# Decoder layer on 8 cores: the mixer's tile loads, tables and out-projection traffic issued from ScalarE's queue, and a second tile buffer for the out-projection

## What is computed

```python
u = modulate(rmsnorm(h, mix_norm), sh2, sc2)
proj = u @ w_in                       # q, k, v of 4 differential heads; latents and k_rope of 4 MLA heads
dq, dk = apply_rope(dq, cos_d, sin_d), apply_rope(dk, cos_d, sin_d)      # tables of 64 columns
kr, q_rope = apply_rope(kr, cos_r, sin_r), apply_rope(q_rope, cos_r, sin_r)  # tables of 32 columns
h = h + g2 * (concatenate([od, om], -1) @ w_out)     # the out-projection
u = modulate(rmsnorm(h, ffn2_norm), sh3, sc3)
h = h + 0.5 * g3 * swiglu(u, w_gate, w_up, w_down)   # D_FF = 2816
```

## Time and profile before

| | us |
|---|---|
| median of 3 executions | 3066.21 (3059.49 to 3182.67) |
| the profiled execution | 3062.68 |
| its span on the slowest core (core 0) | 3061.1 |
| spans of the 8 cores | 3041.2 to 3061.1 |
| PE busy on core 0 | 2843.8 (93%) |
| DVE, ACT busy | 1402.7 (46%), 1255.3 (41%) |

### The profile page before, as it was taken

The page is one execution under the profiler, slowest core; times in us unless marked ns, Lnnn a source line. Parts: engine busy times, 40 slices in busy tenths (PEclk is TensorE's granted clock), DMA queues, the critical chain, the costliest instruction groups (busy, mean ns, idle before and its releaser), DMA issues.

```text
span 3061.1 us, 42691 instructions; the slowest of 8 cores (3041.2 to 3061.1 us)
## 1 busy us (share of the span) xinstructions
PE 2843.8 (93%) x16528; PEld 1355.0 (44%) x16528; DVE 1402.7 (46%) x2808; ACT 1255.3 (41%) x1751; POOL 75.1 (2%) x147
## 2 busy tenths in 40 slices
PE   3999988999899999999978999999999999999998
PEld 1344433444454444544434445544454444444443
DVE  2555215445465445344445545654535444532532
ACT  2421105335434456454235453555755624322311
POOL 1000000000000000000000000000000000000000
PEclk9999999999999999999989999999999999999999
DMA  9678985476924934552793334334245368436446
GB/s 212 116 146 160 201 217 170 125 213 129 205 81 111 180 124 99 121 155 104 234 281 117 97 104 125 111 116 144 75 135 154 119 234 281 138 110 200 165 121 223
DMA packets 144138, 470.76 MB, mean 154 GB/s; under 512 B 17376, under 2 KB 21216, under 8 KB 129760
## 3 DMA queue, kind: packets, MB, share of 16 engines
q1 hardware_dynamic: 127600, 399.80, 41.2%
q0 software_dynamic: 16336, 68.23, 15.0%
HBM read 452.83 MB, written 100.66 MB: 181 GB/s over the span
## 4 chain that ended last, share of the span: by engine, by line
PE 75%; DMA 12%; ACT 5%; DVE 5%; SPq 1%; issue 1%; POOL 0%; ACTq 0%; DVEq 0%; POOLq 0%
PE psall L127 75%; ACT pt L127 3%; DMA hst<-xL 2%; DMA h<-hst 2%; DMA h<-qk 2%; DMA wf<-sdn 2%; SPq L127 1%; DMA wf<-wgu 1%; DMA wf<-w_ada 1%; ACT mu L127 1%; DMA qk<-h 1%; ACT L127 1%; DVE accsb L127 1%; DVE qk L127 1%; DVE mu L127 1%
## 5 line engine op out<-in xcount | busy, mean ns | idle before, releaser
L127 PE MATMUL psall<-uf,wf 128*128 128x512 bf16 x4224 | 1036.7, 384 | 39.7 <-DMA wf<-wgu 13.2
L127 ACT ACTIVATE pt<-psall 128x1024 bf16<-128x1024 f32 (+3 forms) x520 | 452.8, 872 | 458.4 <-PE psall L127 456.9
L127 PEld LDWEIGHTS psall<-uf,wf 128*128 128x128 bf16 x4224 | 399.9, 99 | 472.2 <-issue 36.7
L127 PE MATMUL psall<-actf,wf 128*128 128x512 bf16 x2112 | 514.4, 385 | 16.6 <-DMA wf<-sdn 16.6
L127 ACT ACTIVATE ftf<-psall 128x512 f32<-128x512 f32 x352 | 210.0, 597 | 658.3 <-PE psall L127 638.4
L127 DVE SCALAR_TENSOR_TENSOR ftf<-ftf,psall 128x512 f32<-128x512 f32 x352 | 241.1, 685 | 443.6 <-ACT ftf L127 412.5
L127 PE MATMUL psall<-mu,wm 128*128 128x512 bf16 (+2 forms) x1312 | 328.9, 381 | 13.7 <-ACT mu L127 9.6
L127 PE MATMUL psall<-mixb,wf 128*128 128x512 bf16 x1408 | 323.0, 384 | 9.0 <-ACT mixb L127 6.7
L127 PEld LDWEIGHTS psall<-actf,wf 128*128 128x128 bf16 x2112 | 200.0, 99 | 226.0 <-issue 18.7
L127 DVE SCALAR_TENSOR_TENSOR hst<-psall,SC,hst 128x512 f32<-128x512 f32 x120 | 90.0, 750 | 434.5 <-PE psall L127 260.4
L127 DVE TENSOR_TENSOR actf<-ftf,psall 128x512 bf16<-128x512 f32 x264 | 180.9, 685 | 195.2 <-PE psall L127 192.8
(11 more groups left out here) (113 smaller groups left out, 1993.6 us busy)
## 6 DMA issues: line engine op xcount, KB each, us to landing
wf<-sgu SPq DMA_DIRECT2D x242, 512.0 KB, 4.1
wf<-sdn SPq DMA_DIRECT2D x192, 352.0 KB, 4.2
h<-hst SPq DMA_DIRECT2D x120, 256.0 KB, 4.5
xt<-h SPq DMA_DIRECT2D x30, 1024.0 KB, 7.2
wm<-w_ada POOLq DMA_DIRECT2D x32, 512.0 KB, 11.0
hst<-xL SPq DMA_DIRECT2D x64, 256.0 KB, 7.4
qk<-h SPq DMA_DIRECT2D x16, 1024.0 KB, 6.6
h<-qk SPq DMA_DIRECT2D x16, 1024.0 KB, 9.6
```

The source lines that it names most:

```text
L127: ins = getattr(eng, o.fn[0])(**o.fn[1])
```

## The change

- `load_half` takes an engine. The mixer's loads of tiles 0 to 3 go to ACT's queue. They are not issued at once: `later(n, fn)` puts a function into `posts_m`, and the main loop runs it n lane-M pieces later (`run_posts_m`). Tile 0's halves come 3 and 6 pieces after the mixer's start, the table load 8, tile 1's halves 18 and 21; the prefetches 2 pieces after the piece that frees the half. The lag of the first norm goes from 14 to 20.
- `tables` stores to `tabC`; a new `spread_tab` copies each sample's tables DRAM to DRAM into `tabD` [2, 128, 2, T] and `tabE` [2, 32, 2, T] (8 copies of 128 KB and 4 of 64 KB a sample, on SP, in lane M behind the adaLN products). `load_tab` is then one transfer: 1 MB on ACT, or 256 KB on SP.
- The out-projection has two tile buffers: QK for even tiles, and VA with TAB (`VTP`) for odd ones. Its loads (`oload`) and stores (`ostore`) are on ACT: a store 2 pieces after m = 3 and m = 7, the load of that half for tile tt + 2 five pieces after the store. The ones in VA are written anew by a memset at the start of mixer 1's projection.
- A tile yields 8 x W_OUT, and W_OUT is 1.3 for sample 0 and 0.75 for sample 1; 3 more pieces follow the last tile. The out-projection weights are released two pieces at a time during the last tile.

```diff
-W_OUT = 0.75
+W_OUT = [1.3, 0.75]
...
-    tabD = dscr("tabD", [2, 4, 128, 512], BF16)
+    tabC = dscr("tabC", [2, 128, T], BF16)
+    tabD = dscr("tabD", [2, 128, 2, T], BF16)
+    tabE = dscr("tabE", [2, 32, 2, T], BF16)
...
+        VAF, TABF = VA[:, 0:4096].bitcast(F32), TAB[:].bitcast(F32)
+        VTP = [(VAF[:, k * 512:(k + 1) * 512], vaR) for k in range(4)] + [(TABF[:, k * 512:(k + 1) * 512], tabR[2 * k:2 * k + 2]) for k in range(4)]
+        OUTP = [QKP, VTP]
...
                 if nxt is not None and k % 4 == 3 and nxt[2]():
-                    load_half(pcs, nxt[0], nxt[1], tag, k // 4)
+                    later(2, functools.partial(load_half, pcs, nxt[0], nxt[1], tag, k // 4, (), "act"))
...
+        def later(n, fn):
+
+            posts_m.append([n, fn])
+
+        def run_posts_m(everything=False):
+            due = []
+            for x in posts_m:
+                x[0] -= 1
+                if x[0] <= 0 or everything:
+                    due.append(x)
+            for x in due:
+                posts_m.remove(x)
+                x[1]()
...
+        def spread_tab(s):
+
+            dma_group([tabDR[s]], tabCR[s], f"txd{s}", [(tabD[s, 32 * q:32 * q + 32, si, :], tabC[s, 64 * (1 - si):64 * (1 - si) + 32, :]) for q in range(4) for si in range(2)])
+            yield 6.0
+            dma_group([tabER[s]], tabCR[s], f"txe{s}", [(tabE[s, 16 * q:16 * q + 16, si, :], tabC[s, 32 + 64 * (1 - si):48 + 64 * (1 - si), :]) for q in range(2) for si in range(2)])
+            yield 6.0
...
             if diff:
-                parts = [(slice(32 * r, 32 * r + 32), si, 64 * (1 - si), 32) for r in range(4) for si in range(2)]
+                S.dma("act", r=[tabDR[s]], w=tabR, stream="taba", out=flat, in_=tabD[s])
             else:
-                parts = [(slice(64 + 16 * r, 80 + 16 * r), si, 32 + 64 * (1 - si), 16) for r in range(2) for si in range(2)]
+                S.dma("sp", r=[tabER[s]], w=tabR, stream="tabs", out=flat[64:96], in_=tabE[s])
...
-                                      functools.partial(there, tt), lambda: True, ("mu", s, tt), 14, nxt, True))
-            for tt, pcs, tag in ((0, MIXP, "MIX"), (1, MUS, "MUS")):
+                                      functools.partial(there, tt), lambda: True, ("mu", s, tt), 20, nxt, True))
+            for tt, pcs, tag, n in ((0, MIXP, "MIX", 1), (1, MUS, "MUS", 16)):
                 assert there(tt)
                 for h in range(2):
-                    load_half(pcs, hD[0][s, tt], hR[0][s][tt], tag, h)
+                    later(n + 2 + 3 * h, functools.partial(load_half, pcs, hD[0][s, tt], hR[0][s][tt], tag, h, (), "act"))
+            later(8, functools.partial(load_tab, s, True))
...
+                    if s == 1 and a == 0 and tt == 0:
+                        I("dve", "memset", w=vaR, ap=vaug[:, :, :, 128:129], constant=1.0)
...
+            def ostore(tt, h):
+                ks = range(4 * h, 4 * h + 4)
+                S.dma("act", r=[x for k in ks for x in OUTP[tt % 2][k][1]], w=[hR[1][s][tt][k] for k in ks], stream=f"os{tt % 2}{h}",
+                      out=hD[1][s, tt, :, 4 * h:4 * h + 4, :].rearrange("p k n -> p (k n)"), in_=oflat(tt, h))
+                if h == 1:
+                    flags.add(("h", 1, s, tt))
+                if tt < 2:
+                    later(5, functools.partial(oload, tt + 2, h))
+            for tt in range(2):
+                for h in range(2):
+                    later(2, functools.partial(oload, tt, h))
...
-                    if m in (4, 7):
-                        if m == 7:
-                            yield W_OUT
...
+                    if m in (3, 7):
+                        later(2, functools.partial(ostore, tt, m // 4))
+                    if tt == 3 and m % 2:
+                        wm.release((s, "wo", m // 2))
+                    yield W_OUT[s]
...
+            for _ in range(3):
+                yield W_OUT[s]
...
             for s in range(2):
+                yield from spread_tab(s)
```

More of the change, by code:

```diff
@@ L259, in build @@
         hR = [[[[Res(f"h{i}_{s}_{t}_{k}") for k in range(NK)] for t in range(4)] for s in range(2)] for i in range(3)]
-        tabDR = [[Res(f"tabD{s}_{t}") for t in range(4)] for s in range(2)]
+        tabCR = [[Res(f"tabC{s}_{t}") for t in range(4)] for s in range(2)]
+        tabDR = [Res(f"tabD{s}") for s in range(2)]
+        tabER = [Res(f"tabE{s}") for s in range(2)]
         sguR = [[Res(f"sgu{i}_{j}") for j in range(22)] for i in range(2)]
@@ L359, in dma_group, with load_half @@
                 o.dval = first.dval
[L361 removed]
+        def load_half(pcs, src, srcR, tag, h, after=(), eng="sp"):
             ks = range(4 * h, 4 * h + 4)
@@ L367, in load_half @@
                 out, frm = flat[:, h * 2048:(h + 1) * 2048], src[:, 4 * h:4 * h + 4, :].rearrange("p k n -> p (k n)")
-            o = S.dma("sp", r=[srcR[k] for k in ks] if srcR else [], w=[x for k in ks for x in pcs[k][1]], stream=f"{tag}{h}", out=out, in_=frm)
+            o = S.dma(eng, r=[srcR[k] for k in ks] if srcR else [], w=[x for k in ks for x in pcs[k][1]], stream=f"{tag}{h}{eng}", out=out, in_=frm)
             for q in after:
@@ L765, in tables @@
             yield 2.0
-            S.dma("sp", r=[snR], w=[tabDR[s][tt]], stream="tst", out=tabD[s, tt], in_=sn[:])
+            S.dma("sp", r=[snR], w=[tabCR[s][tt]], stream="tst", out=tabC[s, :, tt * 512:(tt + 1) * 512], in_=sn[:])
+        def spread_tab(s):
[3 more added lines that the diff above has]
+            yield 6.0
         def load_tab(s, diff):
+            flat = TAB[:].rearrange("p (s t) -> p s t", s=2)
             if diff:
-                parts = [(slice(32 * r, 32 * r + 32), si, 64 * (1 - si), 32) for r in range(4) for si in range(2)]
+                S.dma("act", r=[tabDR[s]], w=tabR, stream="taba", out=flat, in_=tabD[s])
             else:
-                parts = [(slice(64 + 16 * r, 80 + 16 * r), si, 32 + 64 * (1 - si), 16) for r in range(2) for si in range(2)]
-            dma_group(tabR, tabDR[s], "tab", [(TAB[rows, si * 2048:(si + 1) * 2048].rearrange("p (t n) -> p t n", t=4),
-                                               tabD[s, :, d0:d0 + n, :].rearrange("t p n -> p t n")) for rows, si, d0, n in parts])
+                S.dma("sp", r=[tabER[s]], w=tabR, stream="tabs", out=flat[64:96], in_=tabE[s])
         evq = collections.deque()
@@ L1148, in mixer, with oflat, oload @@
                 yield W_PROJ
-            def oload(tt):
-                load_tile(QKP, hD[0][s, tt], hR[0][s][tt], "QK")
-            oload(0)
+            def oflat(tt, h):
+                return QK[:].bitcast(F32)[:, h * 2048:(h + 1) * 2048] if tt % 2 == 0 else (TABF if h else VAF)
+            def oload(tt, h):
+                ks = range(4 * h, 4 * h + 4)
+                S.dma("act", r=[hR[0][s][tt][k] for k in ks], w=[x for k in ks for x in OUTP[tt % 2][k][1]], stream=f"ol{tt % 2}{h}",
+                      out=oflat(tt, h), in_=hD[0][s, tt, :, 4 * h:4 * h + 4, :].rearrange("p k n -> p (k n)"))
+            def ostore(tt, h):
+                ks = range(4 * h, 4 * h + 4)
+                S.dma("act", r=[x for k in ks for x in OUTP[tt % 2][k][1]], w=[hR[1][s][tt][k] for k in ks], stream=f"os{tt % 2}{h}",
[7 more added lines that the diff above has]
+                    later(2, functools.partial(oload, tt, h))
             for w in range(4):
@@ L1254, in lane_m @@
             derive(1, "g")
+            for s in range(2):
+                yield from spread_tab(s)
             for s in range(2):
```

19 lines of the change are left out of this document (4 added, 15 removed).

## The result

The change makes the kernel slower: the ratio of its time to the time of the kernel before is 1.0088, with a 95% interval of 1.0064 to 1.0113, where the prediction had 0.9924. On the 3066.2 us of before that is 27 us lost instead of 23 won, and outside the range. The profiled execution took 3095.1 us (before: 3062.7). Of the five executions of the changed kernel three were disturbed, with a lower clock on one half of the chip, so their median (3123.7) says nothing; ratios leave such executions out throughout, and this one rests on the other two.

The account below looks back on a forecast made before the run. PE, 93% busy, bounds the kernel; only its 217 us idle and lower-clock matmuls can change. Gains 32.1 less costs 9 net 23: 3062.7 becomes 3039.7, plus 3.5 gives 3043 us (forecast case 3036 to 3050, range 3026 to 3067).

Parts of the forecast that it names:

- (1): Mixer starts: tables off SP let FFN weights go out earlier, removing PE waits of 5.44 and 8.04, 13.5 us won.
- (3): Out-projections: two tile buffers end the DVE stalls on loads and PE waits of 1.09, 5.55 and 1.75, 8.4 us won.
- rival A: Mixer starts: bandwidth, not the queue, so weight waits and half the clock gain stay; 7 us won, 3059; chance 0.17.
- (2): Mixer 1's start: tiles on ACT, spread over pieces, remove a 4.16 us norm wait; six more lag steps cost nothing.
- (4): Sample 0's out-projection: 18.5 us more FFN filler gains nothing; late FFN2 norms cost 1 us, 5 if it runs over.
- the cover of 8 us for tile 1: Last FFN: tile 1's normalized input was finished at 2587.95 and used at 2595.95, cover expected to be just used up.
- (5): Matmuls after PE gaps run at the lower clock; with the gaps gone 6 us come back, between 0 and 8.
- (6): ACT's queue: issuing 50 transfers takes 16 us of ACT, mostly covered; cost 2 us, between 0 and 16.
- rival D: Out-projections: ACT blocks on its own stores, the stall moves from DVE to ACT; 3056; chance 0.07.
- (7): FFN1's down-projection: 24 new DRAM to DRAM copies on SP cost 6 us, between 0 and 41.
- rival B: FFN1's down-projection: copies hold SP like the table loads, residual loads lack cover, 41 us lost; 3078; chance 0.09.
- The place that the prediction calls the worst: FFN1's down-projection, about 323 to 350 us, DMA engines 0.93 busy: called the worst place for more traffic.

Follow-up runs that it names:

- e4: Kernel before with the table part alone: the copies and one large table load per mixer start, left on SP; ratio 1.0043 to before.
- e5: Changed kernel without copies, lag 14, W_OUT 0.75 for both samples; second tile buffer and spread mixer loads on ACT stay; ratio 0.993 to before.
- e7: As e5, but with all of ACT's transfers (tiles, tables, out-projection) put back on SP at the same places; ratio 0.9938 to before.
- e12: e5 run again unchanged, in five rounds, for a tighter interval; ratio 0.9948 to before.
- e6: e5 with the first norm's lag at 20 instead of 14, so no copies and short fillers; ratio 1.002 to before.
- e11: e5 with one out-projection tile buffer loaded from SP as before; tables and mixer tiles stay on ACT; ratio 0.9977 to before.
- e3: Changed kernel with short fillers, W_OUT 0.75 for both samples instead of 1.3 and 0.75; ratio 1.0026 to before.
- e8: e5 with longer fillers still, W_OUT 1.9 instead of 0.75 for sample 0; ratio 1.0007 to before.
- e1: Changed kernel without the 24 DRAM to DRAM copies; tables load in eight and four pieces, the eight from ACT; ratio 1.0052 to before.
- e10: e5 with copies put back elsewhere (sample 0's in FFN1's gate-up, sample 1's in mixer 0), large table load on ACT; ratio 1.0013 to before.

## Why the prediction was wrong

The sign was wrong. The gains of (1) to (3) came, nearly in the size forecast, though not all by the means named. Three costs failed: the lag was put at nothing, the long fillers at 1 us, and the copies at 6. They measured 22, 19 and 11 us. The 6 us of the clock did not come either.

**(1) Tables off SP, 13.5: half by this step, the rest by another.** "What is behind them on SP goes out 12.8 and 14.9 us earlier": I read the length of eight issues as SP's own work. e4 made them one, and the queue was still held for 5.51 and 8.24 us; the weight waits fell from 15.1 to 7.1 us in the mean of the cores. So the step gave about half of what it promised; for the other half rival A's reading was right, the transfers and not the queue. What took the rest away was the spreading of (2), by which tile 1's halves come after the weights: e5 to e7 have it, and e7 has it with everything on SP and eight issues. The Trainium skill (DMA: Bandwidth & Descriptors, Issuing engines are not separate DMA queues) says that transfers of all issuing engines interleave on the same 16 DMA engines. e7 agrees, as far as two executions tell (0.9938 against 0.993). The prediction set that rule's second half aside because eight issues took 12.81 us; in e7 the same eight take 5.86, so more than half of this number was waiting. As a whole, rival A failed: spread transfers do remove the waits.

**(2) Mixer tiles spread, 4.2 won and the lag at nothing: half right.** In e12 the idle time from the out-projection to mixer 1's first projection matmul is 3.8 us against 19.9, 16.1 less, where (1), (2) and (3) had promised 8.04 + 4.16 + 5.55 + 1.09 = 18.8 on core 0. But "FFN work taken earlier, not added: nothing" is the step that failed for the lag. It measured 22 us (e6 over e12, clear of both intervals), 9 when undone in the changed kernel. The work is the same, but every later DMA issue of lane F moves against lane M by 4.5 us, and an order tuned by hand does not stay tuned: a conversion slid between two adaLN loads. The prediction asked what the moved filler does to PE and never what its transfers collide with.

**(3) Two tile buffers, 8.4: right.** e11 measured 9, with the named waits back. A small slip in its working (eight matmuls at the rate of 20 in 4.48 us are 1.79 us, not 1.73) changes nothing.

**(4) Longer fillers, 1 to 5: the largest miss.** Undone alone, they gave 19 us (e3). I said that the FFN-only part at the end shrinks and that PE is full there anyway, which holds; the cover of 8 us for tile 1 was "just used up", and it ran over, by 3.9 us of waiting and 3.9 of slower matmuls in the mean of the cores, so 8 where 1 was put in the sum and 5 was its upper bound. What I left out is larger: 18.5 us of FFN work moved ahead of mixer 1's start bring another part of the FFN beside its tile and table loads. In the changed kernel it is a down-projection whose weights come late; with 1.9 it is a gate-up phase and costs as much (e8). Weight waits at mixer 1's start are 8.4 us with 1.3, 12.7 with 1.9, and 0.2 in e12. Why the weights come late at just these places was not shown. Which other point of the order would suit is not known.

**(5) Clock, 6 won: the sign was wrong.** With gaps moved and not removed, matmuls took 15 us more in the changed kernel than before (23.1 of length less 8.1 of idle time, mean of the cores), though their number is the same. Where the gaps went (e12), length falls by 13.5 and idle time by 16, so the 6 us don't show in the sum, though the mean granted clock of its executions is 0.986 against 0.984 before. What removed gaps give back stays open within a few us.

**(6) What ACT pays, 2: nothing speaks against it.** Its 48 issues (24 a sample, not 25) hold ACT for 19.1 us, where 16 were estimated. e5 and e7 differ by 0.0008, with up to 0.004 left open. ACT stood behind its own store for 4.24 us before 1581.48 on core 0 of the changed kernel, between two of PE's waits for weights; rival D did not happen.

**(7) Copies, 6 of 0 to 41: too small.** e1 gives 11 us (0.0036) and 14.8 in the stretch where I put them; e10 gives 20 at another place. SP is not held for long, 17.4 us by all 24, so rival B's price (its issue time, 41, and 29 to decide) was wrong. Its picture of residual loads without cover is nearer: PE's waits for `hst` are 11.0 us longer with the copies than without (25.2 against 14.2, mean of the cores). The bandwidth estimate (2.5 MB at 224 GB/s, 11 us, half hidden) was too low at least by the half that it took as hidden. Whether the loads are late because SP was held or because the DMA engines were shared is not separated in the changed kernel; e10 shows some of each. From 320 to 380 us core 0 moved 11.77 MB in the changed kernel and 13.38 in e1, with the DMA engines 0.88 and 0.92 busy, which may be lower throughput or, as PE stood still, lower demand. The place that the prediction calls the worst was the place to price from above.

The sum: e12 is 16 us faster than before and the changed kernel 27 slower, 43 us apart; copies, lag and fillers, undone one at a time, account for 39 of them, each within 10 to 13. Each of the three is also shown on e12's side, clear of its interval: lag 20 costs 22 us, copies at another place 20, and fillers of 1.9 cost 18.

## What to carry to other kernels

A long issue on a queue is not the cost of issuing. Before counting on it, look at what was issued just ahead: if megabytes stand there, fewer issues help in part (half of the waits here), and later ones help more. Spreading large loads, so that the small ones with a near date go first, did the work here; a second queue added nothing that shows. And look at all cores: core 0 alone says that e4 gained next to nothing at mixer 1's start, where the mean of the eight is 4 us.

Filler work that is "only moved" carries its weight loads, conversions and stores with it. In a kernel with a fixed order, follow each of those transfers to its new neighbour before writing zero.

A one-off rearrangement of data in DRAM needs a place where nothing with a near date is queued behind it. The profile shows such loads by what DVE waits for, and not by the busy share of a stage.

## What the runs showed of the hardware

- A single 1 MB table load took 8.24 us to issue on SP behind 4 MB of tile loads (e4); the same kind of issue took 0.33 us on ACT with the tile loads spread (two in the changed kernel, 0.326 and 0.333 us). In this kernel the length of an issue told mostly how much stood ahead of it.
- The 16 DRAM to DRAM copies of 128 KB into `tabD`, issued in 5.18 and 7.33 us for eight, had a median of 13.2 us and a maximum of 26.5 us to landing in a loaded stage, against 1024 KB loads of tiles that landed in 7.5 us in the median over the kernel. In e10 the same 16 copies had a median of 4.3 and a maximum of 15.8.
- One gap of 3.13 us was followed by 61 matmuls at 0.282 us each instead of 0.224, and core 0's window from 2600 to 2650 us had a granted clock of 0.93, where the same window was at 1.00 before.
